# One encoder step on one core: the attention of blocks 2 to 8 moved beside the expert heads, with a row ring of 6

## The chip, the core and the metric

The kernel runs on one core of one Trainium2 chip. A time is microseconds of device time from the start to the end of one execution, and the median of three runs is compared. TensorE (PE) multiplies matrices, VectorE (DVE) and ScalarE (ACT) work element by element, GpSimd (POOL) does small work and writes the descriptors of the gathers, SyncE (SP) issues the other transfers. All transfers of the core run on 16 DMA engines.

## What is computed

One layer over 1024 prompt rows (8 blocks of 128) and 64 sample rows (a ninth block, number 8): attention with a forget gate beside a depthwise convolution, a projection, and then a mixture of experts (PEER) that picks 16 of 16384 experts for each row and each of 8 heads. All in float32. Cut to what matters:

```python
z = rms_norm(x, g_mix) @ w_in
q, k, v, f_logit, a, gate = jnp.split(z, [o1, o2, o3, o4, o5], axis=-1)
logf = jax.nn.log_sigmoid((f_logit + b_f).astype(jnp.float32))
attn = fox_attention(q, k, v, logf, k_past, v_past, logf_past)   # 8 heads of 64, blocks of 128 queries
conv, conv_state = conv_module(a, gate, conv_past, w_dw, b_dw, ln_g, ln_b)   # 31 taps, layer norm, silu
x = x + jnp.concatenate([attn, conv], axis=-1) @ w_out
...
# peer_ffn, for each block of rows xb = rms_norm(x, g_ffn):
q = (xb @ w_pq).reshape(t, PEER_HEADS, 2, PEER_HALF)
s = jnp.einsum('thpd,phkd->thpk', q, keys)
top_s, top_i = lax.top_k(s, PEER_TOPK)
...
h = jnp.einsum('td,thkd->thk', xb, u_emb[expert])
act = (g * jax.nn.gelu(h, approximate=False)).astype(xb.dtype)
return jnp.einsum('thk,thkd->td', act, v_emb[expert])
```

A query block b of the prompt looks at key blocks 0 to b; the sample block looks at a cached block of 128 keys and its own.

## The kernel before

Three phases follow each other, each a block of five engine programs with a barrier at its end. Nothing is scheduled by a tool: the order on each engine is the order of the code, and semaphores join the engines.

**Phase A** (`phase_a`) loops over the nine blocks. PE turns the normed rows and multiplies by the six parts of `w_in` in the order gate, a, f, k, q, v. DVE makes the gated rows `u` and convolves a block with 124 instructions of 128 by 128 (31 taps, 4 chunks, line 577). SP loads the rows of block b+1 into `x` (line 304), ahead of the stores of block b. On ACT, `row_scale(b + 1)` waits for these rows and stands in the program ahead of the sigmoid (line 412) without which `u` of block b can't be made. What phase A makes stays on chip: `keysT`, `values`, `queries`, `convT`.

**Phase B** (`phase_b`) goes through 72 attention heads (9 blocks of 8): scores (line 779) and mask (784) on PE, row maximum on DVE (948), exponential on ACT (883), division by the row sum on DVE (956), turning on PE (794), copy (891, 964), values (808). Beside them it norms the convolution rows (1017 to 1024, POOL 752 to 753), makes the silu gate (a reciprocal of 128 by 512, line 981), and stores the joined result `catT` of each block to HBM (723). POOL convolves the sample block in 31 taps of two instructions (738, 741). The projection and norm of block 0 are done here too (822, 971).

**Phase C** (`phase_c`) goes through 68 expert heads: 8 for each prompt block, and 4 for the sample block, with two heads in one. In an expert head n there are 16 gathers k (line 1220): each brings 128 rows of 8 KB, one expert for each row of the block, into one slot of the ring `uv_rows`, `RING = 8`. DVE multiplies the first half of the row by the normed block (`dot`, line 1582). After two dots ACT makes the gelu (1425), DVE the weight (`act_c`, 1599), ACT two diagonal matrices (1433), and PE adds the second halves of both rows into PSUM (`weigh`, line 1311, 8 matmuls a pair, 16 instructions). POOL issues gather m only when the pair that holds slot m % 8 is weighed: `pool.wait_ge(weighed, (m - RING) // 2 + 1)`. Between them lie the routing of a later head (query 1274, turning 1282, score 1291, and DVE's choice of experts, lines 1517 to 1573, one step after each dot), and, in heads 1 to 3 of a block, the projection (1323), residual and norm of the next block, whose `catT` comes back from HBM. Ahead of the first expert head the 8 parts of `w_pq` (1183), the sub-keys (1188) and block 0 (`xn_c`, 1181) are loaded.

Of the kernel before, what the change touches and what calls it, by code (L numbers as in the profile page):

```python
# [78 lines left out]
def build(nc, x_prompt, x_sample, cache_k, cache_v, cache_logf, state_conv, g_mix, w_in, b_f, w_dw, b_dw,  # L90
# [11 lines left out]


    d.x1 = nc.dram_tensor("x1_rows", (P, s.D), F32, kind="Internal").ap()
    d.xn2 = nc.dram_tensor("xn2_rows", (P, s.D), F32, kind="Internal").ap()
    d.catT = nc.dram_tensor("cat_turned", (s.NB + 1, P, s.DCH, P), F32, kind="Internal").ap()
    with ExitStack() as ctx:
        g = Named()
        g.ident = ctx.enter_context(nc.sbuf_tensor("ident", [P, P], F32))
        g.neg_half = ctx.enter_context(nc.sbuf_tensor("neg_half", [P, 1], F32))  # L110
        g.w_out = ctx.enter_context(nc.sbuf_tensor("w_out_sb", [P, s.DCH, s.D], F32))
        g.ps = ctx.enter_context(nc.psum_tensor("ps", [P, 8, BANK], F32))
        g.cat_stored = [ctx.enter_context(nc.semaphore(f"cat_stored{i}")) for i in range(2)]
        with ExitStack() as mix:
            c = caches(nc, s, mix)
            phase_a(nc, s, d, g, c)
            phase_b(nc, s, d, g, c)
        phase_c(nc, s, d, g)


def caches(nc, s, ctx):

    c = Named()

    def sb(name, shape):
        return ctx.enter_context(nc.sbuf_tensor(name, shape, F32))


    c.keysT = sb("keysT", [s.HD + 1, s.H, s.NKB * P])
    c.values = sb("values", [P, s.NKB, s.DA])  # L130
    c.queries = sb("queries", [P, s.NB + 1, s.DA])
    c.convT = sb("convT", [P, s.CCH, (s.NB + 1) * P])
    c.cum = sb("cum", [P, s.NB + 1, s.H])
    c.vecT = sb("vecT", [P, s.DCH + 3 * s.CCH])

    c.uT = sb("uT_sample", [P, s.CCH, s.TAPS - 1 + s.TS])
    c.tapsT = sb("tapsT", [P, s.CCH, s.TAPS])
    c.k_stored, c.v_stored, c.misc_stored = (ctx.enter_context(nc.semaphore(n)) for n in ("k_stored", "v_stored", "misc_stored"))
    c.g_mix = c.vecT[:, 0:s.DCH]
    c.b_dw, c.ln_g, c.ln_b = (c.vecT[:, s.DCH + i * s.CCH:s.DCH + (i + 1) * s.CCH] for i in range(3))  # L140
    return c


def phase_a(nc, s, d, g, c):
    with ExitStack() as ctx:
        def sb(name, shape):
            return ctx.enter_context(nc.sbuf_tensor(name, shape, F32))

        def sem(name):
            return ctx.enter_context(nc.semaphore(name))  # L150
# [29 lines left out]
        V_HIGH = s.DCH - 2  # L180
        w_v_low = below(2 * s.DA).rearrange("p (c n) -> p c n", n=s.DA)
        w_v = sb("w_v_sb", [P, V_HIGH, s.DA])
        w_in = sb("w_in_sb", [P, s.DCH, s.NIN - s.DA])

        def weights_of(name, i):
            if name == "v":
                return w_v[:, i, :] if i < V_HIGH else w_v_low[:, i - V_HIGH, :]
# [48 lines left out]
        k_stored, v_stored, misc_stored = c.k_stored, c.v_stored, c.misc_stored  # L236
        act_chain, dve_chain, pool_chain = sem("act_chain_a"), sem("dve_chain_a"), sem("pool_chain_a")
# [18 lines left out]
        def _(sp):  # L256
# [7 lines left out]
            def load_weights(name):  # L264
                lo, width = COLS[name]
                if name == "v":
                    sp.dma_start(w_v[:, :, :], w_rows[:, 0:V_HIGH, lo:lo + width]).then_inc(w_here[name], 16)
                    sp.dma_start(w_v_low, w_rows[:, V_HIGH:s.DCH, lo:lo + width]).then_inc(w_here[name], 16)
# [10 lines left out]
            sp.dma_start(c.values[:, s.NB, :], d.cache_v[0, 0].rearrange("t h e -> t (h e)")).then_inc(past_here, 16)  # L279
            for name in ORDER[1:]:  # L280
                load_weights(name)

            def stores(b, kb, k_out, v_out, rows):
                sp.wait_ge(k_ready, b + 2)
                sp.dma_start(k_out, k_aug[0:rows, :, 0:s.HD]).then_inc(k_stored, 16)
                sp.wait_ge(v_ready, b + 2)
                sp.dma_start(v_out, c.values[0:rows, kb, :]).then_inc(v_stored, 16)

            def prompt_stores(b):
                if isinstance(b, int):  # L290
                    v = c.values[:, b, :]
                else:
                    v = c.values[:, bass.ds(b, 1), :].rearrange("p a n -> p (a n)")
                sp.wait_ge(k_ready, b + 2)
                sp.dma_start(k_rows[bass.ds(b * P, P)], k_aug[:, :, 0:s.HD]).then_inc(k_stored, 16)
                sp.wait_ge(v_ready, b + 2)
                sp.dma_start(v_rows[bass.ds(b * P, P), :], v).then_inc(v_stored, 16)

            sp.sem_inc(k_stored, 16)
            k_rows = d.k_prompt[0, 0]  # L300
            v_rows = d.v_prompt[0, 0].rearrange("t h e -> t (h e)")
            with sp.Fori(0, s.NB - 1) as b:
# [17 lines left out]
        def _(pool):  # L320
# [35 lines left out]
            pool.wait_ge(past_here, 48)  # L356
# [14 lines left out]
        def _(act):  # L371
            chain = Chain(act, act_chain)

            def keys_out(kcount, kb):
                act.wait_ge(kT_psum, kcount)
                for i in range(2):
                    src = ps[0:s.HD + 1, KTB + i, :].rearrange("p (h t) -> p h t", t=P)
                    ins = nc.scalar.copy(c.keysT[:, 4 * i:4 * i + 4, bass.ds(kb * P, P)], src)
# [19 lines left out]
            def iteration(b, kb, q_dst, v_dst, cum_dst, prepare_next):  # L398
# [1366 lines left out]
```

## Time and profile before

| | us |
|---|---|
| median of 3 runs (3468.22 to 3472.59) | 3471.99 |
| the profiled execution, first to last instruction | 3471.7 |
| phase A (to 373.6) | 373.6 |
| phase B (373.6 to 632.4) | 258.8 |
| phase C to the first gather (632.4 to 658.9) | 26.5 |
| first to last gather issued (658.9 to 3441.3) | 2782.4 |
| after the last gather was issued | 30.4 |

The profile is one execution, and a view of it gives either groups of instructions (by line, engine and shape), single instructions in order of time, or busy time in a stretch. An engine that idles is shown with what ended its wait.

### The profile page before, as it was taken

How to read it: one execution, taken by the hardware profiler on the slowest of the kernel's cores; microseconds unless marked ns; L12 is line 12 of the kernel's file. 1: busy time of each engine (PE TensorE's matmuls, PEld its weight loads, DVE VectorE, ACT ScalarE, POOL GpSimd, SP SyncE). 2: the span in 40 equal slices, each digit the busy share in tenths (PEclk: the TensorE clock that was granted, in tenths of full speed). 3: DMA queues.
4: the chain of work that ended last, by engine and by line, in shares of the span. 5: the costliest groups of instructions: out<-in, count | busy, mean ns of one | idle time of the engine just before them, and what ended most of it. 6: DMA issues, size and time to landing. Idle time of an engine off the chain costs nothing. (4 is left out here: it accounts for less than half of the span.)

```text
span 3471.7 us, 41167 instructions
## 1 busy us (share of the span) xinstructions
PE 2483.2 (72%) x13379; PEld 1018.3 (29%) x13379; DVE 2488.9 (72%) x6867; ACT 996.6 (29%) x2816; POOL 1454.8 (42%) x1266
## 2 busy tenths in 40 slices
PE   7999889676667666766766676667666766766764
PEld 4444666422222222222222222222222222222221
DVE  4888678677677767776776777777777766767885
ACT  3333444322232222222222222222222222222331
POOL 2333231144444444444444444444444444535443
PEclk9999889798888888888888888878888888888877
DMA  4000200799999999999999999999999999999997
GB/s 154 27 24 21 75 31 19 276 421 421 420 412 419 420 413 418 415 416 417 416 415 416 411 412 418 419 413 416 417 419 414 413 419 416 402 366 421 413 421 328
DMA packets 194557, 1198.43 MB, mean 345 GB/s; under 512 B 31051, under 2 KB 41379, under 8 KB 55102
## 3 DMA queue, kind: packets, MB, share of 16 engines
q0 software_dynamic: 156672, 1140.92, 79.8%
q1 hardware_dynamic: 37694, 55.13, 4.6%
q8 instruction: 99, 1.62, 0.2%
q14 instruction: 92, 0.75, 0.1%
HBM read 1181.14 MB, written 14.84 MB: 344 GB/s over the span
## 5 line engine op out<-in xcount | busy, mean ns | idle before, releaser
L1311 PE MATMUL ps<-uv_rows,diag 64*64 64x512 f32 x8704 | 1355.1, 748 | 898.7 <-ACT diag L1433 896.9
L1220 POOL DMA_INDIRECT uv_rows<-in_uv_emb,experts x1088 | 1287.0, 1183 | 1510.2 <-PE ps L1311 1304.2
L1582 DVE CUSTOM_DVE_ANT_0 uv_rows<-uv_rows,xn_c 128x1024 f32<-128x1024 f32 x1088 | 1332.7, 1225 | 740.1 <-DMA uv_rows<-in_uv_emb,experts 734.7
L1311 PEld LDWEIGHTS ps<-uv_rows,diag 64*64 64x64 f32 x8704 | 325.4, 154 | 1638.8 <-ACT diag L1433 1206.7
L1425 ACT ACTIVATE gelu_c<-dots 128x2 f32<-128x2 f32 x544 | 110.7, 204 | 1754.1 <-DVE dots L1582 1753.9
L1433 ACT ACTIVATE diag<-ident_twice,act_c 128x64 f32<-128x64 f32 x1088 | 319.2, 340 | 286.6 <-DVE act_c L1599 285.9
L1274 PE MATMUL ps<-w_pq_sb,xnT_c 128*128 128x256 f32 x1152 | 350.5, 435 | 1.2 <-ACT xnT_c L1395 1.2
L1274 PEld LDWEIGHTS ps<-w_pq_sb,xnT_c 128*128 128x128 f32 x1152 | 223.0, 211 | 270.5 <-issue 246.8
L577 DVE SCALAR_TENSOR_TENSOR convT<-w_out_sb,tapsT,convT 128x128 f32 (+1 forms) x960 | 252.8, 343 | 0.0
L517 PE MATMUL ps<-w_in_sb,w_out_sb 128*128 128x512 f32 (+1 forms) x656 | 241.7, 524 | 12.2 <-ACT w_out_sb L403 12.2
L339 POOL TENSOR_TENSOR rstd_a<-ms_a,neg_half 128x1 f32<-128x1 f32 x9 | 85.6, 9509 | 181.1 <-ACT ms_a L384 181.1
L517 PEld LDWEIGHTS ps<-w_in_sb,w_out_sb 128*128 128x128 f32 x656 | 113.1, 192 | 130.8 <-issue 112.7
L1599 DVE SCALAR_TENSOR_TENSOR act_c<-gelu_c,gate_inv,gate_exps 128x2 f32<-128x2 f32 x544 | 117.5, 216 | 45.9 <-ACT gelu_c L1425 42.8
L1323 PE MATMUL ps<-w_out_sb,catT_c 128*128 128x512 f32 x256 | 140.7, 637 | 0.0
L1420 ACT ACT_TABLE_LOAD x72 | 92.4, 1283 | 1.3
L1415 ACT ACT_TABLE_LOAD x71 | 91.1, 1283 | 1.3
L1582 DVE DVE_READ_ACCUMULATOR2_ANT dots<- 128x1 f32 x1088 | 89.3, 82 | 0.0
L779 PE MATMUL ps<-keysT,qT_b 65*128 65x512 f32 (+3 forms) x208 | 88.7, 538 | 0.8 <-ACT qT_b L875 0.8
L948 DVE TENSOR_SCALAR_CACHE_REDUCE scores<-ps,cum 128x256 f32<-128x256 f32 (+7 forms) x72 | 56.0, 777 | 41.4 <-PE ps L784 41.1
L883 ACT ACTIVATE probs<-scores,neg_row_max 128x256 f32<-128x256 f32 (+7 forms) x72 | 53.7, 745 | 94.3 <-DVE neg_row_max L950 94.2
L752 POOL TENSOR_SCALAR ln_var<-ln_mv 128x1 f32<-128x1 f32 x9 | 4.1, 453 | 181.1 <-DVE ln_mv L1018 181.1
L794 PE MATMUL ps<-ident,probs 128*128 128x128 f32 x304 | 53.1, 303 | 25.3 <-DVE probs L956 25.2
(208 smaller groups left out, 2100.9 us busy)
## 6 DMA issues: line engine op xcount, KB each, us to landing
uv_rows<-in_uv_emb,experts POOLq DMA_INDIRECT x1088, 12.6
w_in_sb<-in_w_in SPq DMA_DIRECT2D x4, 2048.0 KB, 11.7
w_pq_sb<-in_w_pq SPq DMA_DIRECT2D x8, 1024.0 KB, 12.0
cat_turned<-catT SPq DMA_DIRECT2D x9, 512.0 KB, 2.6
w_out_sb<-in_x_prompt SPq DMA_DIRECT2D x8, 512.0 KB, 3.6
w_out_sb<-in_w_out SPq DMA_DIRECT2D x1, 4096.0 KB, 16.0
catT_c<-cat_turned SPq DMA_DIRECT2D x8, 512.0 KB, 8.0
out<-x_c SPq DMA_DIRECT2D x8, 512.0 KB, 8.2
```

The costliest lines, as they stand in the source:

```text
L517: ins = pe.matmul(ps[:, BANK_OF[name], 0:width], hT[:, i, :], weights_of(name, i), start=(i == 0), stop=(i == s.DCH - 1))
L577: ins = nc.vector.scalar_tensor_tensor(out=dst, in0=src, scalar=c.tapsT[:, i, j:j + 1], in1=dst, op0=ALU.mult, op1=ALU.add)
L1220: nc.gpsimd.indirect_dma_start(out=rows[:, m % RING, :], out_offset=None, in_=d.uv_emb[0], in_offset=bass.IndirectOffsetOnAxis(ap=experts[ ...
L1274: ins = pe.matmul(ps[:, Q_, 0:PAIR], xnT[:, x, :], w_pq[:, x, h * PAIR:(h + 1) * PAIR], start=(x == 0), stop=(x == s.DCH - 1))
L1311: ins = pe.matmul(ps[dst, 2 * x + half, :], diag[src, (m + i) % DIAGS, :], rows[src, (m + i) % RING, cols], start=first, stop=last)
L1323: ins = pe.matmul(ps[:, XT_ + half, :], catT[:, x, :], w_out[:, x, half * BANK:(half + 1) * BANK], start=(x == 0), stop=(x == s.DCH - 1))
L1415: nc.scalar.activation(exps[:, h, :], best[:, r % 2, :], ACT.Exp, bias=nbest[:, r % 2:r % 2 + 1], accum_out=expsum[:, h:h + 1]).then_inc(e ...
L1420: nc.scalar.activation(back[:, :], g.neg_half[:, :], ACT.Gelu).then_inc(gelu_back, 1)
L1425: nc.scalar.activation(gelu[:, n % 2, ks], dots[:, n % 2, ks], ACT.Gelu).then_inc(gelu_ready, 1)
L1433: nc.scalar.mul(diag[:, m % DIAGS, :], ident_twice[:, :], act_w[:, n % 2, k:k + 1]).then_inc(diag_ready, 1)
L1582: nc.vector.tensor_tensor_reduce(out=row, in0=row, in1=xn[:, block_of(n) % 2, :], scale=1.0, scalar=0.0, op0=ALU.mult, op1=ALU.add, accum_ ...
L1599: nc.vector.scalar_tensor_tensor(out=act_w[:, n % 2, ks], in0=gelu[:, n % 2, ks], scalar=gate_inv[:, n % 2:n % 2 + 1], in1=exps[:, slot_of ...
```

## The change

Phase B now does the 16 heads of blocks 0 and 1 alone, with the projection and norm of block 0. The 56 heads of blocks 2 to 8 become items of phase C: item i is done beside expert heads i and i+1. For this phase A writes turned keys, values, queries and convolved rows to HBM (`kT`, `v`, `q`, `conv`), and SP brings them back item by item in phase C. `w_pq` is loaded in phase A, the sub-keys are loaded and turned in phase B, and block 0 is handed on in place. Five large tiles of phases A and C share one area, `handed`. The ring goes from 8 to 6 slots.

```diff
@@ build, phase_a
+    d.kT = nc.dram_tensor("keys_turned", (s.H, s.HD + 1, s.NKB * P), F32, kind="Internal").ap()
+    d.v = nc.dram_tensor("values_by_pair", (s.H // 2, P, s.NB + 1, 2 * s.HD), F32, kind="Internal").ap()
+    d.q = nc.dram_tensor("query_rows", (s.NB + 1, P, s.DA), F32, kind="Internal").ap()
+    d.conv = nc.dram_tensor("conv_turned", (s.NB, P, s.CCH, P), F32, kind="Internal").ap()
...
+            sp.wait_ge(kT_ready, PAST)
+            store_keysT(s.NB)
+            for h in range(s.PH):
+                hs = slice(h * 2 * s.HALF, (h + 1) * 2 * s.HALF)
+                sp.dma_start(g.w_pq[:, :, hs], d.w_pq[0][:, hs].rearrange("(c p) n -> p c n", p=P)).then_inc(g.w_pq_here, 16)
+            for b in range(s.NB - 1):
+                round_of(b)
@@ phase_b
+        FIRST = 2
...
+        TAPS_BEFORE = (0, 5, 17, 25, s.TAPS)
...
+                if i == FIRST:
+                    pool.wait_ge(ss_ready, 1)
@@ phase_c
-        RING = 8
+        RING = 6
...
+            def load_keys(i):
+                b, h = item_of(i)
+                lo = 0 if b < s.NB else s.NB * P
+                sp.dma_start(kT_h[:, 0:keys_of(i)], d.kT[h, :, lo:lo + keys_of(i)]).then_inc(kT_here, 16)
...
+            def head_step(n, k):              # on PE
+                i = n - 1
+                if 0 <= i < ITEMS:
+                    if k == 1:
+                        turn_head_probs(i, 0)
+                    if k == 3 and len(pieces_of(i)) == 2:
+                        turn_head_probs(i, 1)
+                    if k == 5:
+                        weigh_head_values(i)
+                i = n
+                if i < ITEMS:
+                    if k == 7:
+                        head_scores(i, 0)
+                    if k == 11 and len(pieces_of(i)) == 2:
+                        head_scores(i, 1)
...
+            def head_row_max(i, piece):       # on DVE, after dots 9 and 13
+                dve.wait_ge(piece_psum, pieces_before(i) + piece + 1)
...
+            def head_output(i):               # on ACT, after the fourth pair
+                act.wait_ge(pv_psum, i + 1)
...
+                if n % s.H == 6 and k in (4, 6, 8):
+                    conv_gated(n // s.H, (k - 4) // 2)
```

The order on SP at the head of phase A, before (lines 267 and 268 load the last part of `w_in`, 304 the rows of block 1, 295 stores the keys of block 0):

```order
L267 DMA w_v_sb<-in_w_in 128x6x512
L268 DMA w_out_sb<-in_w_in 128x2x512
L302 UNCONDITIONAL_BRANCH
L302 ISA
L304 ISA
L304 DMA w_out_sb<-in_x_prompt 128x1024
L294 REGISTER_ALU
L295 ISA
L295 DMA out<-w_out_sb 1024x1x64
```

The same place in the change (289 is the last part of `w_in`, 327 the rows of block 1):

```order
L289 DMA handed<-in_w_in 128x8x512
L304 DMA keys_turned<-handed 65x8x128
L338 DMA w_pq_sb<-in_w_pq 128x8x256 x8
L327 DMA w_out_sb<-in_x_prompt 128x1024
L315 DMA out<-w_out_sb 1024x1x64
L317 DMA query_rows<-handed 128x512
```

A store and the eight parts of `w_pq` have moved in ahead of the rows of block 1.

The order on PE through one expert head, before (1274 is the query of a later head, 1311 the weighing of a pair, 8 for each pair, 1282 and 1291 the routing's turning and score):

```order
L1274 MATMUL ps<-w_pq_sb,xnT_c 128x256 x2
L1311 MATMUL ps<-uv_rows,diag 64x512 x8
L1274 MATMUL ps<-w_pq_sb,xnT_c 128x256 x2
L1311 MATMUL ps<-uv_rows,diag 64x512 x8
L1282 MATMUL ps<-ident,q_c 128x128 x2
L1311 MATMUL ps<-uv_rows,diag 64x512 x8
L1291 MATMUL ps<-sub_keysT,qT_c 128x128 x2
L1311 MATMUL ps<-uv_rows,diag 64x512 x24
```

The same engine in the change, in an expert head beside an item of block 7 (8 key blocks; 1374 weighs a pair, 1334 is the query, 1481 turns the item's probabilities, 1497 its values, 1461 its scores in two pieces):

```order
L1481 MATMUL ps<-ident,head_scores 128x128 x4
L1374 MATMUL ps<-uv_rows,diag 64x512 x8
L1334 MATMUL ps<-w_pq_sb,xnT_c 128x256 x2
L1497 MATMUL ps<-pair_values,head_probsT 128x64 x8
L1374 MATMUL ps<-uv_rows,diag 64x512 x8
L1334 MATMUL ps<-w_pq_sb,xnT_c 128x256 x2
L1461 MATMUL ps<-head_keysT,pair_queriesT 128x512
L1374 MATMUL ps<-uv_rows,diag 64x512 x8
L1342 MATMUL ps<-ident,q_c 128x128 x2
L1374 MATMUL ps<-uv_rows,diag 64x512 x8
L1354 MATMUL ps<-handed,qT_c 128x128 x2
L1461 MATMUL ps<-head_keysT,pair_queriesT 128x512
```

The item's matmuls stand between the weighings of five of the eight pairs.

## Rows read from the trace of the kernel before

**Rows 1.** The page, transfers by queue: packets, MB, share of 16 engines' span.

```profile
q0 software_dynamic: 156672, 1140.92, 79.8%
```

**Rows 2.** Stretches: us; busy PE, PEld, DVE, ACT, POOL; granted clock; DMA share; GB/s.

```profile
0.00:373.60 373.60, 341.68 (x1179) 177.12 (x1179) 277.39 (x1035) 129.05 (x262) 99.58 (x75) 1.00 0.17 54
373.60:632.40 258.80, 223.33 (x1440) 161.81 (x1440) 186.90 (x462) 121.04 (x289) 55.24 (x84) 0.86 0.11 42
632.40:658.90 26.50, 17.97 (x84) 14.93 (x84) 9.03 (x40) 5.30 (x13) 0.41 (x2) 0.78 1.08 335
658.90:3441.30 2782.40, 1889.32 (x10612) 661.86 (x10612) 1999.30 (x5304) 735.97 (x2237) 1297.90 (x1104) 0.85 1.01 415
```

**Rows 3.** The 1088 gathers of line 1220: from issue to landing.

```profile
DMA to landing us min/median/max: 9.1/12.6/27.3
```

**Rows 4.** Timeline of one expert head: start us, us, engine, line [idle before it].

```profile
1511.95 1.23 DVE L1582 CUSTOM_DVE_ANT_0 uv_rows<-uv_rows,xn_c 128x1024 f32<-128x1024 f32 x1 [1.08 <-DMA uv_rows<-in_uv_emb,experts]
...
1514.36 3.61 PE L1311 MATMUL ps<-uv_rows,diag 64*64 64x512 f32 x16 [1.86 <-ACT diag L1433]
...
1514.42 1.23 DVE L1582 CUSTOM_DVE_ANT_0 uv_rows<-uv_rows,xn_c 128x1024 f32<-128x1024 f32 x1 [0.74 <-DMA uv_rows<-in_uv_emb,experts]
...
1516.90 1.23 DVE L1582 CUSTOM_DVE_ANT_0 uv_rows<-uv_rows,xn_c 128x1024 f32<-128x1024 f32 x1 [0.65 <-DMA uv_rows<-in_uv_emb,experts]
...
1518.78 0.94 POOL L1220 DMA_INDIRECT uv_rows<-in_uv_emb,experts  x1 [4.79 <-PE ps L1311]
...
1519.55 1.95 PE L1311 MATMUL ps<-uv_rows,diag 64*64 64x512 f32 x16 [1.22 <-ACT diag L1433]
...
1521.80 0.94 POOL L1220 DMA_INDIRECT uv_rows<-in_uv_emb,experts  x1 [0.37 <-PE ps L1311]
```

**Rows 5.** The same view and head: PE's query behind a weighing.

```profile
1506.74 1.13 PE L1274 MATMUL ps<-w_pq_sb,xnT_c 128*128 128x256 f32 x4
```

**Rows 6.** Timeline at the start of phase C.

```profile
637.15 1.97 PE L1261 MATMUL ps<-ident,xn_c 128*128 128x128 f32 x8 [7.70 <-DMA xn_c<-xn_rows]
637.26 19.50 SPq L1183 DMA_DIRECT2D w_pq_sb<-in_w_pq  x7
...
658.93 1.24 POOL L1220 DMA_INDIRECT uv_rows<-in_uv_emb,experts  x1 [26.11 <-DVE experts L1573]
...
668.21 1.23 DVE L1582 CUSTOM_DVE_ANT_0 uv_rows<-uv_rows,xn_c 128x1024 f32<-128x1024 f32 x1 [1.64 <-DMA uv_rows<-in_uv_emb,experts]
```

**Rows 7.** The page, DMA issues by line: times, KB of each, median us to landing.

```profile
cat_turned<-catT SPq DMA_DIRECT2D x9, 512.0 KB, 2.6
...
catT_c<-cat_turned SPq DMA_DIRECT2D x8, 512.0 KB, 8.0
```

**Rows 8.** Timeline at the head of phase A, block 0.

```profile
27.20 0.91 SPq L304 DMA_DIRECT2D w_out_sb<-in_x_prompt  x1
...
38.00 1.06 ACT L383 ACTIVATE w_out_sb<-w_out_sb 128x1024 f32<-128x1024 f32 x1 [14.75 <-DMA w_out_sb<-in_x_prompt]
...
41.32 0.69 DVE L552 TENSOR_TENSOR w_out_sb<-ps,w_out_sb 128x512 f32<-128x512 f32 x1 [38.44 <-ACT w_out_sb L412]
...
46.27 0.60 PE L527 MATMUL ps<-ident,w_out_sb 128*128 128x128 f32 x4
```

**Rows 9.** Timeline of phase B, blocks 1 and 2.

```profile
408.99 0.72 POOL L741 TENSOR_TENSOR convT<-tapped,convT 128x256 f32<-128x256 f32 x1
...
410.49 0.73 POOL L741 TENSOR_TENSOR convT<-tapped,convT 128x256 f32<-128x256 f32 x1
...
410.64 1.06 PE L862 MATMUL ps<-ident,z_b 128*128 128x128 f32 x4
...
412.85 0.66 PE L808 MATMUL ps<-probsT,values 128*64 128x128 f32 x8
...
414.58 7.03 PE L822 MATMUL ps<-w_out_sb,catT 128*128 128x512 f32 x16
```

**Rows 10.** Group of phase B: count, busy us, mean ns, idle before.

```profile
L981 DVE RECIPROCAL silu_gate<-silu_gate 128x512 f32<-128x512 f32 x9 | 30.2, 3352 | 0.3
```

More of the change, by code:

```diff
@@ new lines, in _ @@
+            first = c.first
+            sp.wait_ge(kT_stored, 16 * 4)
+            sp.dma_start(first.keysT[:, :, :], d.kT[:, :, 0:2 * P].rearrange("h e t -> e h t")).then_inc(c.first_here, 16)
+            sp.wait_ge(q_stored, 16 * 3)
+            sp.dma_start(first.queries[:, :, :], d.q[0:2].rearrange("b p n -> p b n")).then_inc(c.first_here, 16)
+            sp.wait_ge(v_stored, 32 * 3)
+            for kb in range(2):
+                sp.dma_start(first.values[:, kb, :].rearrange("p (c n) -> p c n", n=2 * s.HD),
+                             d.v[:, :, kb, :].rearrange("c p n -> p c n")).then_inc(c.first_here, 16)
@@ L309, in _ @@
+            sp.wait_ge(conv_stored, 16 * 3)
+            sp.dma_start(first.convT[:, :, :, :], d.conv[0:2].rearrange("b p c t -> p b c t")).then_inc(c.first_here, 16)
+            last = s.NB - 1
+            stores(last, last, k_rows[last * P:s.NB * P], v_rows[last * P:s.NB * P, :], P)
             sp.wait_ge(u_ready, 1 + s.NB)
@@ L680, in at @@
-        def at(n):
-            return min(units(n)) * BANK
-        def turned_at(n):
-            return min(turned_units(n)) * BANK
-        def weighed_before(n):
-            return max(n - n % 2 - 2, 0)
-        def heads_before(n, places):
-            return max([m + 1 for m in range(n) if places(m) & places(n)], default=0)
-        def wide_before(n):
-            return sum(wide(m) for m in range(n))
-        def ahead(n):
-            far = n + 3
-            near = n < 0 or not wide(n)
-            return min(far if near and not wide(min(far, HEADS - 1)) else n + 2, HEADS - 1)
@@ L863, in _ @@
                     ins.then_inc(zT_psum, 1)
[L864 to L866 removed]
+                if b == 1 and h in (5, 6):
+                    project(h - 5)
             weigh_values(HEADS - 2)
+            for i in range(2):
+                turn_keys(i)
         @block.scalar
@@ L933, in _ @@
                     silu_exp(b - 1)
-                if h == 6 and b == s.NB:
-                    silu_exp(b)
-            outputs_out(BLOCKS - 1)
+            silu_exp(FIRST - 1)
+            stage_stored(act)
+            outputs_out(FIRST - 1)
+            for i in range(2):
+                keys_out(i)
         @block.vector
@@ L1289, in score @@
                     pe.wait_ge(s_out, r)
+                if issued.values:
+                    pe.wait_ge(o_ready, issued.values)
+                issued.scores += 1
                 for p in range(2):
@@ new lines, in turn_head_probs @@
+            def turn_head_probs(i, piece):
+                lo, hi = pieces_of(i)[piece]
+                if piece == 0:
+                    pe.wait_ge(p_ready, i + 1)
+                    if i % 2 == 1:
+                        pe.wait_ge(qT_h_ready, (i + 1) // 2 + 1 if i + 1 < ITEMS else ITEMS // 2)
+                    if i % s.H == 2:
+                        pe.wait_ge(y_out, i // s.H + 1)
+                    if i % s.H == 4:
+                        pe.wait_ge(yn_ready, i // s.H + 1)
+                    if i % s.H == 0 and i > 0:
+                        pe.wait_ge(oT_ready, i // s.H)
+                else:
+                    pe.wait_ge(turned_ready, pieces_before(i) + piece)
+                for x in range(lo, hi, P):
+                    ins = pe.transpose(ps[:, B_, x - lo:x - lo + P], scores[:, x:x + P], g.ident[:, :])
+                ins.then_inc(turned_psum, 1)
@@ L1346, in _ @@
+            issued = Named()
+            issued.scores, issued.values = 0, 0
+            for half in range(2):
+                turn_rows(0, half)
             query(0)
-            pe.wait_ge(keys_here, 32)
-            turn_keys(0)
             for r in range(FIRST_ROUTED):
                 turn_query(r)
-                if r == 0:
-                    pe.wait_ge(keys_ready, 1)
                 score(r)
                 query(r + 1)
-                if r == 0:
-                    turn_keys(1)
@@ L1454, in _ @@
+            for half in range(2):
+                rows_out(0, half)
             for r in range(FIRST_ROUTED):
                 query_out(r)
-                if r < 2:
-                    keys_out(r)
                 turned_out(r)
+                if r == 2:
+                    head_queries_out(0)
                 if r == 3:
```

898 lines of the change are left out of this document (568 added, 330 removed).

## The prediction

> **What bounds the kernel now.** I read the busy time by stage first. Between the first and the last gather lie 2782.4 us of the 3471.7, and there the DMA engines are busy all the time (share 1.01, 415 GB/s) while PE is busy for 68% and DVE for 72% [rows 2]. The queue of the gathers carries 1140.92 MB [rows 1], 1088 gathers of 1.05 MB, so one passes every 2782.4 / 1088 = 2.557 us. In the timeline of one expert head the reader is to see that dots follow each other at 2.48 us, that each waited for its transfer, and that PE, ACT and POOL follow behind [rows 4]. So this stage is bound by bytes, and nothing that the other engines do in it shows. Phase B is the opposite: 258.8 us with the DMA engines at 0.11 [rows 2]. Phases A and B hide none of the gathers.
>
> **Phase B.** It goes from 72 heads to 16. Head 13 of 16 turns its normed convolution rows at 410.64 [rows 9]. From there: to 411.5; projection half 0, 16 instructions, 7.03 [rows 9]; head 14's part about 1.1 (its values 0.66 [rows 9]); half 1, 7.0; so PE is done with it near 426.7. Residual and mean square on DVE and the root on POOL are about 2.8 (each instruction of DVE here 0.7 to 1.2, as the residual of 0.69 [rows 8] and the dot of 1.23 [rows 4], whose shapes they have), and POOL then still has 6 of the 31 taps, at 410.49 - 408.99 = 1.50 each [rows 9], 9.0. With 0.9 for the barrier phase C starts near 439.5 instead of 632.4: **-193**. It may be 5 more or less. The sub-keys' turning and the norm of block 0 end inside these 9 us and cost nothing while the taps are last.
>
> **Start of phase C.** PE began 4.8 us in, when `xn_c` had come [rows 6]; now the block is in place. Some 0.8 of copying sub-keys also goes. **-5**.
>
> **Start of phase A.** This is what the early query weights cost. The rows of block 1 were issued at 27.20 and were there at 38.00, behind all of `w_in`; ACT waited 14.75 for them, and ahead of the sigmoid; DVE made `u` at 41.32 to 42.0, PE turned it at 46.27 [rows 8], so 4.3 us were spare. In the change eight parts of `w_pq` go ahead of these rows on SP. Seven took SP 19.50 us to issue [rows 6], so eight take 22.3 and the rows can't be issued before 49.5; and 8.4 MB at 335 GB/s [rows 2] take 25 us of the engines, so they land near 63.8, 25.8 later. Less the 4.3: **+21.5**. PE is busy for 341.7 of phase A's 373.6 us [rows 2], so it doesn't win this back. Ends: 49.5 + 2.6 [rows 7] = 52, which is +10, and +28. The new stores of phase A wait for nothing late: the DMA share there is 0.17 [rows 2].
>
> **Bytes.** The items read keys 9.3 MB (65 rows of 4 bytes for 4224 keys and 8 heads, and the sample's), values 9.0, queries 1.8 and conv rows 1.6: 21.8 MB. The 8 loads of `catT_c`, 4.2 MB [rows 7], go. 17.6 MB at 415 GB/s [rows 2]: **+42**. The Trainium skill (DMA: Bandwidth & Descriptors, section on why a DMA increments its semaphore by 16) says that a DMA from SP runs on the largest number of engines up to 16 that divides its rows; 65 rows would run on 13. No row here shows a DMA of 65 rows; by it the keys would take 16/13 of their time, 5 us more.
>
> So far 3471.7 - 193 - 5 + 21.5 + 42 = **3337**. Everything left is loss in phase C, where bytes no longer bound if the ring is too short.
>
> **The ring of 6.** A pair of slots goes round once in three pairs. By bytes alone a round may take 6 x 2.557 = 15.34, and with the new bytes (42 us over 1088 / 6 = 181 rounds) 15.57 us. What a round needs: from the first dot of a pair to the second 2.48; from the second to the next issue of the slot, 1516.90 to 1521.80, 4.90, with a weighing of 1.95; or 1511.95 to 1518.78, 6.83, with one of 3.61 [rows 4]. Those are the two levels of PE's clock, 2.4 and 1.2 GHz; the granted clock is 0.85 over the stage [rows 2], so 30% of the time is at the lower one. Then the time from issue to landing. With 8 slots it is 12.6 in the median, most of it queue, and 9.1 at least [rows 3]; that minimum has other gathers ahead of it, and so does the 9.28 of the first (658.93 to 668.21), with query weights under way [rows 6]. So 9.1 is the upper end for a gather alone. The lower end is a 512 KB store, 2.6 [rows 7], plus 1.25 for the other half MB at 415 GB/s, plus POOL's 0.94 [rows 4]: 4.8. I take 6.8, about the middle, since neither row is nearer. A round then needs 2.48 + 4.90 + 6.8 = 14.2 or 16.1, and 14.8 in the mean: it fits, with little over.
>
> **The items' work between the weighings.** At the full clock a pair leaves PE 5.1 - 1.95 - 1.13 = 2.0 us [rows 4, 5], and the item's pieces fit: 4 turnings about 0.5, scores 0.9 a piece (2 of the 16 instructions of 7.03 [rows 9]), values of 8 blocks about 2. At the lower level each doubles: 3.6 + 2.3 is already over 5.1, and five pairs are late by 1.4, 1.4, 3.7, 2.2 and 1.9. At 30% that is 3.2 a head. DVE's row maximum stands behind dot 9 and waits for scores that PE then does 4 late, with the next dots queued behind it: 1.2 a head. ACT's exponential and its wait for the values: 0.7. Together 5.1 over 8 pairs, 0.64 each. The projection, now beside values and scores in two heads of eight, and a reciprocal of 3.35 [rows 10] in one of eight: 0.29. Mean round 14.8 + 0.9 = 15.7 against 15.57. If slack of fast rounds could be kept for slow ones, the loss were 0.12 x 181 = 22 us. It can't, once the DMA engines have idled: with all 5.1 falling on the slow pairs a slow round is 16.1 + 2.2 = 18.3, 2.7 short, and 0.3 x 149 rounds of the 56 heads give 121. Slow stretches are shorter than a round or two, so I stay under that and take **+109** in all.
>
> **Sum:** 3337 + 109 = **3446**, 0.7% under the profiled execution, which is the median within 0.3 us.
>
> **Rivals.**
> 1. The ring hides everything: a lone gather lands in 5 to 6 us. For it: queueing explains all of 12.6. Against: nothing in 1088 gathers is under 9.1 [rows 3]. A slow round is then 16.1 - 1.4 + 0.9 = 15.6, as long as the bytes: 3337 + 15 = **3352**. The Trainium skill (the same page, section Anatomy of one DMA, SWDGE path) gives about 2.0 us plus bytes over 436 GB/s for one, so 4.4 here. The trace has none under 9.1, though none alone.
> 2. Slower: landing sets the round. It decides from the point where a mean round is 15.57 + 134.7 / 181 = 16.31, which is a landing of 7.4 us. At 7.8 the mean round is 16.7, 1.1 x 181 = 203, with about 35 for the slow stretches: **3575**. For it: the minimum of 9.1, and the item's loads of up to half a MB that come in front of gathers. Against: those are already counted as bytes.
> 3. The early weights delay nothing, because SP's transfers overtake each other: 3446 - 21.5 = **3425**. Against: the rows of block 1 came only after 14.75 us of waiting [rows 8].
>
> **How the numbers follow.** The forecast, losses of 60 to 160 (3400 to 3500), has 0.42; rival 1 0.20, rival 2 0.28, rival 3 0.10. A measurement of this kernel can tell about 0.2%, 7 us, from no change. Of the forecast's part 0.25 is faster, 0.08 same, 0.09 slower; rival 3 is faster but for 0.01: faster 0.54, same 0.08, slower 0.38. The forecast's own range is 3400 to 3500; the range that should hold 8 in 10 goes from rival 1 to rival 2: 3352 to 3580. A landing of 9.1 would give over 3700 and is left outside.
>
> **What would show it.** Phase B of 66 us; the wait of ACT at the head of phase A about 26 longer, and all of phase A longer by some 20; the DMA share of the gather stage under 1.0 and the rate under 415 GB/s; the median from issue to landing down from 12.6 to 7 or 8; POOL's waits for the weighing no longer than before while DVE's waits for gathers grow. If the DMA share stays at 1.0, rival 1 holds; if waits for `ps` of the scores on DVE lead, the items and not the ring are the loss. I am wrong if phase A keeps its length, or if a lone gather takes under 6 or over 7.4 us.

## The result and the profile after

The changed kernel takes 3595.44 us in the median (3589.59 to 3610.35), the kernel before 3471.39: a ratio of 1.0365, 95% interval 1.0343 to 1.0388. It is 3.6% slower. The prediction said 3446, between 3352 and 3580. Its own profiled execution takes 3591.7 us.

The stretches of the changed kernel, in the columns of [rows 2]: phase A, phase B, phase C to the first gather, the gathers, the rest.

```profile
0.00:396.00 396.00, 343.81 (x1179) 177.96 (x1179) 276.12 (x1032) 128.74 (x262) 96.98 (x75) 0.98 0.32 101
396.00:464.40 68.40, 48.90 (x216) 32.62 (x216) 37.28 (x101) 23.02 (x69) 46.04 (x69) 0.75 0.27 93
464.40:484.85 20.45, 17.42 (x70) 13.63 (x70) 8.69 (x37) 3.76 (x9) 0.42 (x2) 0.81 0.25 84
484.85:3564.20 3079.35, 2115.27 (x11894) 849.58 (x11894) 2106.96 (x5668) 861.23 (x2576) 1273.90 (x1119) 0.84 0.98 380
3564.20:3591.70 27.50, 10.27 (x48) 2.17 (x48) 13.09 (x20) 3.62 (x10) 1.47 (x2) 0.57 0.31 114
```

| stage | before | after | difference | predicted |
|---|---|---|---|---|
| phase A | 373.6 | 396.0 | +22.4 | +21.5 |
| phase B | 258.8 | 68.4 | -190.4 | -193 |
| phase C to the first gather | 26.5 | 20.45 | -6.05 | -5 |
| first to last gather | 2782.4 | 3079.35 | +296.95 | +42 +109 |
| the rest | 30.4 | 27.5 | -2.9 | 0 |

So the first gather leaves 174 us earlier, as foretold, and the whole miss, 146 us, lies between the first and the last gather. There the rate fell from 415 to 380 GB/s, while the DMA share is still 0.98. The reader should note how little that share says: it counts the time that packets take, and the packets took longer. A packet of 8 KB took 0.317 us in the mean in the kernel before and 0.335 in the changed one; of the first 16 packets of a gather, 0.315 and 0.360. The rate is what shows the loss.

The line of the gathers in the changed kernel: what POOL waited for before it issued one, who waited for the rows, and issue to landing.

```profile
  PE ps L1374: 1536.1, 502
...
  DVE experts L1823: 102.6, 16
...
  DVE uv_rows L1832: 856.7, 853
...
DMA to landing us min/median/max: 5.5/9.0/19.1
```

Before, the median landing was 12.6 and the least 9.1 [rows 3]. Now it is 9.0 and 5.5: less stands in the queue. And DVE waits longer for rows. Fifteen of the 16 waits put down to the choice of experts stand at the first gather of a head: it is issued 0.8 us after the weighing that frees its slot, where other pairs follow some 0.3 after theirs. So they are the same wait for the ring, with at most 0.5 us each of their own.

The chain of waits of the changed kernel, a piece near its end (start, us, what), shows a round of the ring whole:

```profile
3492.29 3.73 PE ps L1374 x16
3496.02 0.26 issue
3496.28 1.28 POOL uv_rows L1270
3497.56 0.30 issue
3497.87 9.53 DMA uv_rows<-in_uv_emb,experts
3507.46 1.11 issue
3508.57 0.09 DVE dots L1832
3508.69 0.21 ACT gelu_c L1611
3508.93 0.23 DVE act_c L1849
3509.18 0.59 ACT diag L1619 x2
3509.78 0.04 issue
3509.82 3.63 PE ps L1374 x16
```

A pair is weighed, POOL issues the two gathers into its slots (1.28 and the next), the second lands 9.53 after its issue, the dot, gelu, weight and diagonals follow, and the pair is weighed again: 3509.82 - 3492.29 = 17.53 us for six gathers. Six gathers at the rate of before take 15.34. No engine is busy throughout, and at 380 GB/s for 415 the DMA engines aren't used in full either; the loop of waits is the bound.

### The profile page after: what moved, and what is told of

Same layout as the page of the kernel before. It is cut to its first block and busy times, and to the rows that moved or that the text cites. A ratio compares the mean times of both kernels' runs of the same rounds, so it can differ in the third digit from the quotient of the medians.

```text
span 3591.7 us, 41643 instructions
## 1 busy us (share of the span) xinstructions
PE 2535.7 (71%) x13407; PEld 1076.0 (30%) x13407; DVE 2442.1 (68%) x6857; ACT 1020.4 (28%) x2925; POOL 1418.8 (40%) x1266
## 5 line engine op out<-in xcount | busy, mean ns | idle before, releaser
L1374 PE MATMUL ps<-uv_rows,diag 64*64 64x512 f32 x8704 | 1381.8, 761 | 967.7 <-ACT diag L1619 966.8
L1270 POOL DMA_INDIRECT uv_rows<-in_uv_emb,experts x1088 | 1255.6, 1154 | 1823.9 <-PE ps L1374 1536.1
L1832 DVE CUSTOM_DVE_ANT_0 uv_rows<-uv_rows,handed 128x1024 f32<-128x1024 f32 x1088 | 1331.9, 1224 | 862.6 <-DMA uv_rows<-in_uv_emb,experts 856.7
L626 DVE SCALAR_TENSOR_TENSOR handed<-w_out_sb,tapsT,handed 128x128 f32<-128x128 f32 x960 | 252.8, 343 | 0.0
L1390 PE MATMUL ps<-w_out_sb,handed 128*128 128x512 f32 x256 | 142.2, 639 | 0.0
L1932 DVE TENSOR_SCALAR_CACHE_REDUCE head_scores<-ps,cum 128x512 f32<-128x512 f32 (+2 forms) x88 | 56.2, 639 | 61.5 <-PE ps L1463 38.4
L1461 PE MATMUL ps<-head_keysT,pair_queriesT 65*128 65x512 f32 (+3 forms) x176 | 80.8, 542 | 0.0
L1354 PEld LDWEIGHTS ps<-handed,qT_c 128*128 128x128 f32 x288 | 50.8, 247 | 81.0 <-issue 78.2
L1497 PEld LDWEIGHTS ps<-pair_values,head_probsT 128*128 128x128 f32 x560 | 72.5, 194 | 3.4
L1497 PE MATMUL ps<-pair_values,head_probsT 128*128 128x64 f32 x560 | 69.2, 271 | 0.0
```

What stands on the lines that cost most here:

```text
L626: ins = nc.vector.scalar_tensor_tensor(out=dst, in0=src, scalar=c.tapsT[:, i, j:j + 1], in1=dst, op0=ALU.mult, op1=ALU.add)
L1270: nc.gpsimd.indirect_dma_start(out=rows[:, m % RING, :], out_offset=None, in_=d.uv_emb[0], in_offset=bass.IndirectOffsetOnAxis(ap=experts[ ...
L1374: ins = pe.matmul(ps[dst, 2 * x + half, :], diag[src, (m + i) % DIAGS, :], rows[src, (m + i) % RING, cols], start=first, stop=last)
L1390: ins = pe.matmul(ps[:, X_, :], catT[:, x, :], w_out[:, x, half * BANK:(half + 1) * BANK], start=(x == 0), stop=(x == s.DCH - 1))
L1497: ins = pe.matmul(ps[:, S_, at:at + s.HD], probsT[:, x // 4, (x % 4) * P:(x % 4 + 1) * P], v_pair[:, x, (h % 2) * s.HD:(h % 2 + 1) * s.HD] ...
L1832: nc.vector.tensor_tensor_reduce(out=row, in0=row, in1=xn[:, block_of(n) % 2, :], scale=1.0, scalar=0.0, op0=ALU.mult, op1=ALU.add, accum_ ...
```

## Experiments

For several runs I give the three terms of a round as the trace shows them, a mean over all its pairs (540 or so in each kernel, first gather to last): **release** from the second dot of a pair to the next issue into its slots; **landing** from that issue, the first of the two that POOL then makes, to its dot; **gap** from there to the dot that closes the round. The three terms of one round add up to it by their definition, so the table tells where a round's time lies; what makes the round long is for the runs to show.

| kernel | slots | release | landing | gap | round | round / slots |
|---|---|---|---|---|---|---|
| before | 8 | 5.66 | 12.27 | 2.56 | 20.49 | 2.56 |
| before_ring7 | 7 | 5.57 | 9.80 | 2.56 | 17.93 | 2.56 |
| before_ring6 | 6 | 5.79 | 8.46 | 2.61 | 16.86 | 2.81 |
| before_ring4 | 4 | 6.17 | 6.84 | 2.93 | 15.94 | 3.98 |
| before_ring6_early | 6 | -0.98 | 13.75 | 2.56 | 15.33 | 2.56 |
| changed kernel | 6 | 5.75 | 8.63 | 2.63 | 17.01 | 2.84 |
| after_no_items | 6 | 5.76 | 8.43 | 2.61 | 16.80 | 2.80 |
| after_ring7 | 7 | 5.59 | 10.32 | 2.77 | 18.68 | 2.67 |
| after_ring7_no_items | 7 | 5.54 | 9.83 | 2.59 | 17.96 | 2.57 |

**The ring alone** (before_ring6). A new tile `unused` keeps the room of the two slots, so that every other tile lies where it did.

```diff
-        RING = 8
+        RING = 6
...
+        unused = sb("unused_rows", [P, 8 - RING, 2 * s.D])
```

> The kernel before with RING = 6 and nothing else changed (the freed 16 KB of each partition stay allocated, so every other tile lies where it did). Theory (the ring alone makes the loss): in the changed kernel a round of six gathers takes 17.05 us in the last eight expert heads, which have no item, as in those with one; the same round here gives 1088 / 6 x 17.05 = 3092 us between the first and the last gather instead of 2782, so about 3780 in all. Rival (the items' work makes most of it, the ring of 6 is covered to within the 0.12 us of a round of the prediction's sum): about 3490 to 3530.

Measured: 3749.74 us, ratio 1.0815 (1.0798 to 1.0831). The kernel before, 3469.51 us beside it, loses 280 us by its two slots alone; the theory had 3780 us, the rival 3490 to 3530. The stretch of its gathers:

```profile
655.50:3711.30 3055.80, 1992.39 (x10628) 684.78 (x10628) 2004.62 (x5309) 736.66 (x2240) 1238.97 (x1105) 0.81 0.97 378
```

Its timeline through one round (POOL's issues and DVE's dots, with a weighing):

```profile
1914.02 1.23 DVE L1583 CUSTOM_DVE_ANT_0 uv_rows<-uv_rows,xn_c 128x1024 f32<-128x1024 f32 x1 [1.78 <-DMA uv_rows<-in_uv_emb,experts]
...
1916.42 3.02 PE L1312 MATMUL ps<-uv_rows,diag 64*64 64x512 f32 x16 [1.77 <-ACT diag L1434]
...
1919.73 1.25 POOL L1221 DMA_INDIRECT uv_rows<-in_uv_emb,experts  x1 [2.41 <-PE ps L1312]
1921.29 0.94 POOL L1221 DMA_INDIRECT uv_rows<-in_uv_emb,experts  x1 [0.30 <-issue]
...
1928.06 1.22 DVE L1583 CUSTOM_DVE_ANT_0 uv_rows<-uv_rows,xn_c 128x1024 f32<-128x1024 f32 x1 [0.72 <-DMA uv_rows<-in_uv_emb,experts]
...
1930.51 1.23 DVE L1583 CUSTOM_DVE_ANT_0 uv_rows<-uv_rows,xn_c 128x1024 f32<-128x1024 f32 x1 [0.81 <-DMA uv_rows<-in_uv_emb,experts]
```

The dot at 1914.02 is the second of its pair. Its slots are given back and issued at 1919.73 (5.71), those rows are multiplied at 1928.06 (8.33), and 2.45 later the round is closed: 16.49. There is no item in this kernel, so the items are not needed to explain the loss.

**The items taken out** (after_no_items). ITEMS = 0, and with it the loads, matmuls, row maxima, exponentials and convolution norms of blocks 2 to 8; the first loads of items and the waits for their results go too. The projection of these blocks runs on whatever lies in `catT`.

```diff
-        ITEMS = s.H * (BLOCKS - FIRST)
+        ITEMS = 0
...
```

> The changed kernel with the attention and convolution norm of blocks 2 to 8 left out (no loads, no matmuls, no vector work of the items; the projection still runs on what lies in catT), ring of 6. Theory (the ring alone): the stage is bound by the round and not by bytes, so the 21.8 MB of the items don't come back in full; 0 to 45 us less than the changed kernel, 3550 to 3595. Rival (the items' work costs): 3337 - 52 of bytes + a small ring loss, so 3400 or less.

Measured: 3566.30 us, ratio 1.0283 (1.0263 to 1.0302). That is 29 us under the changed kernel, so all the work and bytes of 56 items cost 29 us at six slots. The prediction had 42 for bytes (net of `catT_c`) and, in its forecast, 0.9 of each round for the items' work. The loss stays when they go.

**One slot less than before** (before_ring7), again the number and the tile that keeps the room.

```diff
-        RING = 8
+        RING = 7
...
```

> The kernel before with RING = 7. Theory (what a round needs is set against what the slots' transfers take): seven gathers take 17.9 us, more than the 16.9 that a round needs, so bytes bound: 3470 to 3490. Rival (each slot less costs about the same, as it would if the loss were only in stretches of the low clock): half of ring 6's loss, about 3610.

Measured: 3474.15 us, ratio 1.0014 (1.0004 to 1.0023). One slot costs 0.14%, the second 8%. It is a threshold, not a slope.

**Four slots** (before_ring4), one execution.

```diff
-        RING = 8
+        RING = 4
...
```

> The kernel before with RING = 4, two pairs of slots. It measures the landing when little else is queued. In before_ring6 a round of 16.9 us is 5.75 from a pair's second dot to the next issue, 8.5 from the issue of the pair's first gather to its dot and 2.6 between the dots; of the 8.5, the transfers still ahead of it at its issue end 4.25 later. Theory (8.5 is 5.5 to 6 of landing alone and the rest queue): a round of two pairs is 5.75 + 5.8 + 2.6 = 14.1, so 1088 / 4 x 14.1 = 3835 for the gathers and about 4520 in all. Rival (8.5 is what a landing costs in any case): 1088 / 4 x 16.9 = 4597, about 5290.

Measured: 5020.37 us, between the theory's 4520 and the rival's 5290. Here a gather can be seen that has nothing ahead of it. The timeline of its gathers and dots:

```profile
2405.50 1.22 DVE L1583 CUSTOM_DVE_ANT_0 uv_rows<-uv_rows,xn_c 128x1024 f32<-128x1024 f32 x1 [0.89 <-DMA uv_rows<-in_uv_emb,experts]
2407.30 0.95 POOL L1221 DMA_INDIRECT uv_rows<-in_uv_emb,experts  x1 [9.11 <-PE ps L1312]
...
2408.55 0.94 POOL L1221 DMA_INDIRECT uv_rows<-in_uv_emb,experts  x1 [0.30 <-issue]
...
2410.24 0.95 POOL L1221 DMA_INDIRECT uv_rows<-in_uv_emb,experts  x1 [0.75 <-PE ps L1312]
2411.80 0.95 POOL L1221 DMA_INDIRECT uv_rows<-in_uv_emb,experts  x1 [0.61 <-issue]
2413.05 1.22 DVE L1583 CUSTOM_DVE_ANT_0 uv_rows<-uv_rows,xn_c 128x1024 f32<-128x1024 f32 x1 [5.73 <-DMA uv_rows<-in_uv_emb,experts]
2415.54 1.23 DVE L1583 CUSTOM_DVE_ANT_0 uv_rows<-uv_rows,xn_c 128x1024 f32<-128x1024 f32 x1 [1.09 <-DMA uv_rows<-in_uv_emb,experts]
...
2418.02 1.23 DVE L1583 CUSTOM_DVE_ANT_0 uv_rows<-uv_rows,xn_c 128x1024 f32<-128x1024 f32 x1 [0.76 <-DMA uv_rows<-in_uv_emb,experts]
...
2420.49 1.23 DVE L1583 CUSTOM_DVE_ANT_0 uv_rows<-uv_rows,xn_c 128x1024 f32<-128x1024 f32 x1 [0.63 <-DMA uv_rows<-in_uv_emb,experts]
```

The ring had run empty (the last dot was at 2405.50). The gather of 2407.30 is multiplied 5.75 later: that is a lone landing. The trace has 257 gathers that were issued after the last packet of the one ahead; the median of their landings is 5.72. The three behind this one take 6.99, 7.78 and 8.69, since they come off the queue at one each 2.47 to 2.49. My theory's landing (5.5 to 6 alone) is seen, but its sum was too low: the mean landing in this kernel is 6.84, because only the first of a pair is ever alone, and the release grew too, from 5.66 to 6.17. PE was busy for 51% of this stretch (68% before) and ran more of it at the lower of its two levels, 1.2 GHz (granted clock 0.70 against 0.85):

```profile
656.90:4988.90 4332.00, 2209.05 (x10644) 733.32 (x10644) 2005.70 (x5313) 736.36 (x2243) 1133.17 (x1104) 0.70 0.70 267
```

**The release taken out of the round** (before_ring6_early), one execution. The weighing reads a tile that lies in place (`w_out`) and not the gathered rows, so the kernel leaves out the sum over the experts; and a slot is given back after its own dot.

```diff
-                    pool.wait_ge(weighed, (m - RING) // 2 + 1)
+                    pool.wait_ge(dot_done, m - RING + 1)
...
-                                            rows[src, (m + i) % RING, cols], start=first, stop=last)
+                                            g.w_out[src, i, half * BANK:(half + 1) * BANK], start=first, stop=last)
```

> The kernel before with RING = 6, where the weighing reads a resident tile instead of the gathered rows (so the sum of the expert outputs is not computed from them) and a slot is given back after its dot instead of after its weighing: the 5.75 us leave the round and everything else stays. Theory (the round is a sum of three terms, any of which can be cut): 16.9 - 5.75 = 11.2 is below the 15.34 that six transfers take, so it is bound by bytes again, 3465 to 3485. Rival (six gathers in flight are too few to keep the DMA engines busy, whatever gives the slots back): 3650 or more.

Measured: 3466.37 us. Its stretch of gathers:

```profile
657.60:3433.00 2775.40, 1878.00 (x10612) 659.54 (x10612) 1997.92 (x5305) 736.65 (x2238) 1080.71 (x1104) 0.85 1.01 416
```

And its gathers from issue to landing:

```profile
DMA to landing us min/median/max: 11.7/13.4/18.5
```

All of the 280 us are back with the same six slots. The release is -0.98 us in the table, since the first slot of a pair is now free after the first dot, ahead of the second from which the release is counted. Six gathers in the ring are enough to keep the DMA engines busy, if the slots aren't held for a weighing: the time that the release leaves free is filled by landing, 13.75 in place of 8.46, which is queue.

**The early query weights** (after_wpq_late).

```diff
-            for h in range(s.PH):
-                hs = slice(h * 2 * s.HALF, (h + 1) * 2 * s.HALF)
-                sp.dma_start(g.w_pq[:, :, hs], d.w_pq[0][:, hs].rearrange("(c p) n -> p c n", p=P)).then_inc(g.w_pq_here, 16)
             for b in range(s.NB - 1):
                 round_of(b)
+                for h in range(2 * b - 2, 2 * b):
+                    if 0 <= h < s.PH:
+                        hs = slice(h * 2 * s.HALF, (h + 1) * 2 * s.HALF)
+                        sp.dma_start(g.w_pq[:, :, hs], d.w_pq[0][:, hs].rearrange("(c p) n -> p c n", p=P)).then_inc(g.w_pq_here, 16)
```

> The changed kernel with the eight parts of w_pq issued two by two behind the stores of blocks 1 to 4 instead of all ahead of block 1's rows. Theory (the prediction's +21.5): phase A is back to about 374 us and the whole is 18 to 25 us shorter, about 3572. Rival (the start of phase A is not what lengthened it; the new stores or turnings are): within 5 us of the changed kernel.

Measured: 3585.96 us, ratio to before 1.0333 (1.0314 to 1.0352). That is 9.5 us less than the changed kernel, under the 18 to 25 of the theory, and the interval overlaps that of the changed kernel, so the medians alone don't decide. The traces do. First the changed kernel at the head of phase A (the parts of `w_pq`, the rows of block 1, ACT's and PE's wait):

```profile
27.07 25.14 SPq L338 DMA_DIRECT2D w_pq_sb<-in_w_pq  x8
...
52.25 2.82 SPq L327 DMA_DIRECT2D w_out_sb<-in_x_prompt  x1
...
62.52 1.06 ACT L434 ACTIVATE w_out_sb<-w_out_sb 128x1024 f32<-128x1024 f32 x1 [34.95 <-DMA w_out_sb<-in_x_prompt]
...
66.59 1.12 PE L578 MATMUL ps<-ident,w_out_sb 128*128 128x128 f32 x4 [15.17 <-DVE w_out_sb L600]
```

Then the same place with the weights late:

```profile
27.64 3.17 SPq L327 DMA_DIRECT2D w_out_sb<-in_x_prompt  x1
...
38.74 1.06 ACT L435 ACTIVATE w_out_sb<-w_out_sb 128x1024 f32<-128x1024 f32 x1 [11.67 <-DMA w_out_sb<-in_x_prompt]
```

The rows are there at 38.74 in place of 62.52. The end of phase A is read from the first instruction on PE in phase B, in the changed kernel and then in this one:

```profile
396.50 1.03 PE L778 MATMUL ps<-ident,first_queries 128*64 128x128 f32 x4 [5.71 <-PEq L164]
...
378.77 1.03 PE L779 MATMUL ps<-ident,first_queries 128*64 128x128 f32 x4 [5.75 <-PEq L164]
```

It comes 17.7 us earlier, and the first gather 15.8 (469.1 against 484.85). But it isn't back at 373.64, where the kernel before has it: 5.1 of phase A's growth have another cause. Most of that lies at the very start, in ACT's copy of the cached keys and PE's first projection, before and in the changed kernel:

```profile
18.70 1.06 ACT L378 COPY keysT<-ps 65x512 f32<-65x512 f32 x2 [1.47 <-PE ps L479]
21.50 24.94 PE L517 MATMUL ps<-w_in_sb,w_out_sb 128*128 128x512 f32 x64 [1.13 <-ACT w_out_sb L403]
...
23.02 1.07 ACT L429 COPY handed<-ps 65x512 f32<-65x512 f32 x2 [6.07 <-SPq L333]
25.82 25.60 PE L568 MATMUL ps<-w_in_sb,w_out_sb 128*128 128x512 f32 x64 [5.74 <-ACT w_out_sb L454]
```

In the changed kernel this copy waits for `kT_stored`, a semaphore that says that the area is free. SP raises it itself once at the start (line 333), but the line stands behind the issue of all of `w_in`, which ends at 22.8. So ACT waits 6.07 us (1.47 before, for PE), though the area has been free from the start, and PE's first projection starts 4.3 later. With the weights late it still starts at 25.31. By these rows, raising the semaphore ahead of the loads would give about 4 us back, an estimate; no run does it.

**A seventh slot in the changed kernel** (after_ring7). The room for it comes from two tiles that can share another's place.

```diff
-        RING = 6
+        RING = 7
...
-        probsT = sb("head_probsT", [P, 2, BANK])
...
-        z = sb("conv_rows", [P, s.DC])
+        z = conv_in[:, :, :].rearrange("p c t -> p (c t)")
...
-                nc.scalar.copy(probsT[:, piece, 0:hi - lo], ps[:, B_, 0:hi - lo]).then_inc(turned_ready, 1)
+                nc.scalar.copy(scores[:, lo:hi], ps[:, B_, 0:hi - lo]).then_inc(turned_ready, 1)
```

> The changed kernel with RING = 7. The room comes from two tiles: the turned probabilities are written back into head_scores, and the normed convolution rows share conv_in. Theory (the ring): with a seventh slot a round of 17.05 us has 7 x 2.595 = 18.2 us of transfers, so bytes bound the stage again: 3337 to 3380. Rival (the items): under 1% faster than the changed kernel, 3560 or more.

Measured: 3394.42 us, ratio 0.9780 (0.9765 to 0.9795): 201 us less than with six slots, and 2.2% faster than the kernel before. The rival is out. It is 14 above the upper end of what the theory gave: the stage takes 2878.7 us at 406 GB/s, where bytes alone would take 2824.

```profile
487.50:3366.20 2878.70, 2036.57 (x11894) 826.69 (x11894) 2100.01 (x5665) 861.25 (x2573) 1282.52 (x1118) 0.87 1.01 406
```

**The items at seven slots** (after_ring7_no_items): the edits of after_ring7 and after_no_items together.

```diff
-        ITEMS = s.H * (BLOCKS - FIRST)
+        ITEMS = 0
...
-        RING = 6
+        RING = 7
```

> after_ring7 with the attention and convolution norm of blocks 2 to 8 left out, as in after_no_items. With six slots leaving them out gave 29 us back. Theory (with seven slots the items are a cost of their own, since the stage is close to bound by bytes): after_ring7 needs 42.9 us for an expert head with an item and 40.2 for one without, so 56 x 2.7 = 150 less would be all of it, of which 52 are bytes; 3394 - 100 to 150 = 3245 to 3295. Rival (those heads are longer for another reason, the clock or the routing, and only bytes come back): 3335 to 3350.

Measured: 3300.39 us, ratio 0.9510 (0.9494 to 0.9526), 94 us less than after_ring7, just short of the theory's 100 to 150.

```profile
489.30:3271.00 2781.70, 1897.46 (x10628) 668.71 (x10628) 2003.62 (x5329) 737.00 (x2240) 1259.52 (x1105) 0.84 1.01 413
```

The same items that cost 29 us where the round bound cost 94 where bytes bind. Of these 21.8 MB / 415 GB/s = 53 are bytes. The other 41 are work between weighings, or transfers of up to half a MB in front of a gather; no run here separates them, nor the bytes from the rest. The prediction also cites a rule for the loads of keys with 65 rows, that they would run on 13 engines (the Trainium skill, DMA: Bandwidth & Descriptors, section on why a DMA increments its semaphore by 16). These loads have no landing time in the profile, so no run here shows it. The changed kernel with eight slots was not run.

**Both mended** (after_ring7_late): the diffs of after_ring7 and after_wpq_late together, the seventh slot and `w_pq` late.

> The changed kernel with RING = 7 as in after_ring7 and w_pq issued behind blocks 1 to 4 as in after_wpq_late. Theory: 3394 less the 16 us by which after_wpq_late issued its first gather earlier: 3370 to 3382. Rival (the loads of w_pq spread over phase A delay the stores there): no faster than after_ring7, 3390 to 3400.

Measured: 3378.83 us, ratio 0.9735 (0.9721 to 0.9748). It is 2.65% faster than the kernel before, inside the theory's 3370 to 3382, and clear of after_ring7 by its interval; so the 16 us of the weights are there in the end as well. Its stretch of gathers starts at 468.0 and runs at the same 406 GB/s.

## Why the prediction was wrong

**What held.** That bytes bound before and leave no room; phase B (-190.4 for -193); the start of phase C (-6.05 for -5); and that the early weights hold back the rows of block 1, which were there at 62.52 where 63.8 was given (its own 38.0 and 25 make 63.0; the prediction doesn't say where the other 0.8 comes from). Rival 3 (SP's transfers overtake each other) is out. The terms outside the gathers sum to -177 where -176.5 was forecast.

**What held by luck.** Phase A grew by 22.4 for 21.5, but the weights are 17.7 of it (after_wpq_late), and the other 5, of which ACT's wait for SP at the start makes about 4, stand in the prediction as nothing. The two errors belong together: it counted 4.3 of slack for PE, from 42.0 to 46.27, and PE in the changed kernel would have got there only at some 50.2, as it does with the weights late. So the slack was 4 larger, and the phase was 4 longer for another reason.

**The step that failed** is the landing in "The ring of 6": "for a gather alone ... I take 6.8". Two things went wrong in it.

The first is the question asked. The prediction looked for the landing of a gather *alone*, and put the point from which the change is slower, rival 2, at a landing of 7.4. A lone gather takes 5.75 (before_ring4), under the 6 that was given as a sign of being wrong and as rival 1 said, and still it was rival 2 that came true. In a ring of three pairs a gather is never alone. In before_ring6, when the first gather of a pair is issued, the one ahead of it still has 4.25 us to go (mean over its pairs; the packets of the trace in order of their start, 128 to a gather); its own last packet comes 2.74 after that one, and its dot 1.47 later: 8.46. Landing is not a constant of the chip that one can put into the sum. It depends on how many are in flight: 6.84, 8.46, 9.80 and 12.27 for 4, 6, 7 and 8 slots.

The second is how far ahead of its turn a gather must be issued so that the DMA engines lose nothing. For this the packets give an estimate. In before_ring6, where the issue came 2.5 to 3.5 us before the last packet of the gather ahead (168 gathers), that packet and the next gather's last one lie 3.21 apart; where it came 4.5 to 5 ahead (172), 2.56. In this starved kernel longer leads don't help further (2.67 at 5 to 6, 2.91 at 6 to 8); 402 of those 559 are second gathers of a pair. In the kernel before, which has a queue, it is 3.02 at 2.5 to 3.5 (22 gathers), 2.70 at 3.5 to 4, and 2.5 to 2.6 from 4 on. Taking 4 to 4.5 us, the landing at full rate is at least that + 2.5 + 1.3 (from the last packet to the dot, its median) = 7.8 to 8.3. With 5.8 for the release and 2.6 for the gap a round needs 16.2 to 16.7 us. Six slots allow 15.34: too short by 0.9 to 1.4, where 1.5 was measured. Seven allow 17.9 and eight 20.5: enough. Without the release it is some 10 against 15.34: enough. All four fall on the side that was measured (2.81, 2.56, 2.56 and 2.56 us for a gather). That this lead is what a gather needs is worked out from the packets of two kernels; no run changes it by itself. The Trainium skill (DMA: Bandwidth & Descriptors, section Anatomy of one DMA, SWDGE path) puts one DMA at about 2.0 us and bytes over 436 GB/s, which for this size is an estimate of 4.4. The lone gather here took 5.75 from the start of its issue to the dot, and neither is the landing that counts in a loop.

**In the sum.** Mean round forecast 15.7 (2.48 + 5.48 + 6.8 + 0.93), measured 17.01 (2.63 + 5.75 + 8.63). The landing is 1.8 short, more than the whole difference, since the 0.93 for items stood beside it; the release was taken from single rows and the clock as 5.48, and is 5.66 over all pairs of the kernel before. The row for the upper level was short (4.90, where 259 pairs have 5.46 in the mean), the one for the lower level right (6.83 for 6.84, 39 pairs). Against 15.57 the measured round is 1.44 too long, and 1.44 x 181 = 261: 3337 + 261 = 3598, near the 3591.7 of the profiled execution. So the form of the sum was right. Two of its terms were not, and they lean against each other: the landing 1.8 too short and the items' work 0.8 too long.

**The items' work** was over-priced where it was put, and for the wrong place. 0.93 of a round stood for it; between before_ring6 and the changed kernel the round differs by 0.15. At six slots all 56 items cost 29 us, so their work mostly falls into waits that are there anyway. The +109 of the forecast was right in neither part: 22, and 87 more for slow stretches that can't be made up, instead of a plain 261 that every round pays.

**The signs that were given.** Phase B took 68.4 us for 66. ACT's wait at the head of phase A grew from 14.75 to 34.95, 20.2 for 26. The median landing was to go down from 12.6 to 7 or 8; it went to 9.0. POOL's waits for the weighing were to stay; the same view of the kernel before has 1304.2 us in 507 waits where the changed one has 1536.1 in 502, so each got longer. DVE's waits for gathers were to grow; they did, from 734.7 in that view to 856.7. The DMA share did fall under 1.0, but only to 0.98, which alone would have looked like rival 1; the rate, 380 for 415 GB/s, tells.

The chance of 0.28 for slower by rival 2 was the right mechanism with the right sign. That its own figure of 3575 was only 0.6% low is in part luck: it took a landing of 7.8, and with the measured 8.6 its sum, items and all, would have given some 3720. What spoke for it in the rows was the least landing of 9.1 among 1088, which the prediction called an upper end.

## What to carry to other kernels

When a ring of buffers is shortened, write down the loop (release, issue, landing, use), and put in the landing that goes with full use of the transfer engines, not that of a lone transfer: compare slots times the time of one transfer with that sum, and expect a threshold. Here the two slots that were given up were worth 280 us, more than the 190 us of attention that was hidden, and a single slot found in two tiles that could be shared turned +3.6% into -2.2%. A transfer queued ahead of one that the first engine waits for costs its time less the slack there, even in a phase where the DMA engines are mostly idle: here rows that came 23.8 us later made the phase 17.7 longer. Move it behind. The same holds for a semaphore that a queue raises itself: put it ahead of the loads that it doesn't depend on.

## What the runs showed of the hardware

- The share of busy DMA engines hides a starved queue: 0.97 at 378 GB/s (before_ring6) and 1.01 at 416 (before_ring6_early). In before_ring6 a gather stretches over 3.37 us from first to last packet in the mean, in the kernel before over 2.90.
- A lone gather of 128 rows of 8 KB takes 5.75 us from issue to use; behind others, one follows each 2.47 to 2.49 us (before_ring4).
- The loop is longer where PE's granted clock is lower. In the kernel before, the release is 5.46 us where the clock was at its upper level at both ends (259 pairs) and 6.84 at the lower (39). With four slots the granted clock was 0.70 and the release 6.17, with six 0.81 and 5.79, with eight 0.85 and 5.66.
- The price of a piece of work depends on what binds: the items cost 29 us at six slots and 94 at seven.
